# Expert weights in pieces of 4 KB a partition, empty places passed over, and one gate product moved, in a one-core stream step

## The chip, the cores and the metric

The kernel runs on one core of a Trainium2 chip. The metric is the device time of one execution in microseconds (us). The kernel before took 2080.77 us, the median of 3 runs (2078.91 to 2081.96). One further execution was profiled: 2079.63 us by the same clock, with a span of 2077.8 us from its first instruction to its last. All times of single instructions below count from the start of that span.

A core has TensorE (PE, with its weight loads shown apart as PEld), VectorE (DVE), ScalarE (ACT), GpSimd (POOL) and SyncE (SP), which run side by side and wait for each other by semaphores, and 16 DMA engines, which all queues share. SP's transfers run in queue q1, POOL's in queue q0.

## The reference, cut to what matters

One layer over 1,088 tokens of 1,024 features (1,024 tokens of a prompt and 64 of a running stream): a state-space branch and a sparse attention branch, gated and projected, a layer norm, and then the mixture of experts, which is what the change touches:

```python
def moe(x, w_router, router_bias, w_exp_gu, w_exp_down, w_sh_gu, w_sh_down):
    scores = sigmoid(xt @ w_router)
    _, idx = top_k(scores + router_bias, 6)              # 6 of 64 experts a token
    gate = take(scores, idx); gate = gate / gate.sum(-1) * 2.5
    routed = routed_experts(xt, idx, gate, w_exp_gu, w_exp_down)
    shared = swiglu(xt, w_sh_gu, w_sh_down)              # silu(x @ w[:, :256]) * (x @ w[:, 256:]) @ w_down
    return routed + shared

def routed_experts(...):
    # token-slots sorted by expert; each expert's rows padded to whole blocks of 128 rows;
    # each block: swiglu(x_pad[tok], w_exp_gu[e], w_exp_down[e]) * g, added to the tokens' rows
```

An expert has a gate-and-up matrix of 1024 x 512 and a down matrix of 256 x 1024, all float32: 2 MB and 1 MB. There are 1088 x 6 = 6,528 token-slots. They don't fill their blocks: a block of 128 rows holds **places**, and those without a token are empty.

## The kernel before

All activations stay in one large tensor in SBUF, `arena`; names such as `xg`, `ewg` and `x1` are slices of it, so a profile shows them all as `arena`. The program is written out engine by engine, in the order in which each is to work, with the semaphores by hand. There is no scheduler.

**Ahead of the expert loop.** After the first layer norm the routing is counted: `count` and `rank` give each token-slot its number among its expert's; a few small DVE steps turn the counts into the experts' first blocks (`blocks_planned`). Beside that runs the shared expert for each of the 9 token tiles i: PE `shared_up(i)` (L845, 16 matmul instructions), ACT takes silu of the gate half (`hsh`), DVE `gate_shared(i)` (L2186) multiplies it by the up half in PSUM, PE turns the product (`turn_hidden`, L827), ACT copies it, PE `shared_down(i)` (L836), and DVE `add_shared(i)` (L2203) adds it to `x1`. PE's results go to PSUM banks that are handed out in turn; PE may fill a bank only when the reader of its former content is done. DVE's loop over i also does, at i = 0, `slots` for tiles 0 to 4, at i = 1 `slots` for tiles 5 to 8 and `block_and_place`, and from i = 2 to 4 one-hot rows for 54 pairs of a tile and a choice (L2304, L2305); POOL makes a third of each pair's rows (L1277), PE multiplies the rows into a table (L891), `tab`, of 128 places x blocks: token and gate of each place. Twelve buffers hold the one-hot rows.

**Empty places.** A place with no token gets the row number T + partition = 1088 + partition in `tab`. `x1_d` and `acc_d` in DRAM have T + 128 rows, so an empty place reads one of 128 spare rows and adds its (zero-gated) result to one.

**The expert loop** runs over blocks in pairs; buffers are doubled by u = 0, 1, and `last_pair` and the experts of the blocks are read from tables. Per block n:

- SP (`load_gu`, `load_dn`, both by `ld`, so the profile's line is L954) loads the 2 MB for block n + 3 when PE has finished gate-and-up of block n + 1, and the 1 MB for block n + 2 when PE has finished the down product of block n. A partition's share is contiguous in DRAM: 16 KB and 8 KB.
- POOL, in this order: four gathers (L1293) of 128 quarter rows of 1 KB each for block n + 3, by DVE's list `tid`; then `scatter` (L1287), which adds 128 rows of 4 KB to `acc_d`. The scatter waits for both halves of the result (`y_half`) and for the landing of the scatter before it (`y_stored`), since two scatters could add to the same row.
- DVE: the list for the next gather (L2258), the gate-and-up product (L2314), the transposes of the gathered rows (L2264, four), two small columns (L2319, L2320), and one half of the weighting of the result (L2323).
- PE: gate-and-up of block n + 1 (L918, 16 instructions), down of block n (L932, 8), the turn of the hidden rows (L924, 2).

After the loop SP waits for both last scatters, loads `acc_d` back and the second layer norm runs tile by tile.

Of the kernel before, what the change touches and what calls it, by code (L numbers as in the profile page):

```python
# [34 lines left out]
T = SEQ + DEC  # L35
NT = 9
DK = DM // P
# [75 lines left out]
def layer_program(nc, a, out):  # L113
    banks = Banks()
    with ExitStack() as ctx:
# [178 lines left out]
        def s(name):  # L294
            if name not in S:
                S[name] = sem(name)
            return S[name]
# [104 lines left out]
        def _(pe):  # L402
# [531 lines left out]
                    last.then_inc(s(f"edn_full{j}"), 1)  # L934

            pe.wait_ge(s("base_ready"), NT)
            gate_and_up(0, 1, 16)
            turn_eh(0, 1)
            with pe.Fori(0, last_pair) as ip:
                for u in range(2):  # L940
                    n = ip * 2 + u
                    gate_and_up(1 - u, n + 2, ip * 16 + 16 + 16 * u)
                    down(u, n + 1, ip * 16 + 16)
                    turn_eh(1 - u, n + 2)
            gate_and_up(1, last_pair * 2 + 2, last_pair * 16 + 16)
            down(0, last_pair * 2 + 1, last_pair * 16 + 16)
            turn_eh(1, last_pair * 2 + 2)
            down(1, last_pair * 2 + 2, last_pair * 16 + 16)


        @block.sync
        def _(sp):
            def ld(dst, src, name, small=False):
                sp.dma_start(dst, src, allow_slow_non_contiguous=small).then_inc(s(name), 16)  # L954
# [156 lines left out]
                return sp.value_load(brow[0:1, bass.ds(n, 1)], min_val=0, max_val=NE - 1)  # L1111

            def load_gu(e, u):
                ld(ewg[u], a["w_exp_gu"][0, bass.ds(e, 1)].rearrange("a (p k) f -> (a p) k f", k=DK), f"ewg_loaded{u}")

            def load_dn(e, u):
                ld(ewd[u], a["w_exp_down"][0, bass.ds(e, 1)].rearrange("a (p k) f -> (a p) k f", k=2),
                   f"ewd_loaded{u}")

            for u in range(2):  # L1120
                e = expert(u)
# [9 lines left out]
            with sp.Fori(0, last_pair) as ip:  # L1131
                for u in range(2):
# [3 lines left out]
                    load_gu(after, 1 - u)  # L1136
                    sp.wait_ge(s("edn_full1"), n + 1)
                    load_dn(e, u)
            sp.wait_ge(s("ewg_loaded0"), last_pair * 16 + 32)
            for u in range(2):  # L1140
                sp.wait_ge(s(f"y_stored{u}"), last_pair * 16 + 32)
            for i in range(NT):
# [15 lines left out]
        def _(pool):  # L1158
# [125 lines left out]
            pool.wait_ge(s("x1_stored"), 16 * NT)  # L1284

            def scatter(u, rows_):
                pool.indirect_dma_start(acc_d, bass.IndirectOffsetOnAxis(ap=sid[u][:, 0:1], axis=0), rows_, None,  # L1287
                                        compute_op=ALU.add).then_inc(s(f"y_stored{u}"), 16)

            def gather(u):  # L1290

                for g in range(4):
                    pool.indirect_dma_start(xg[u][:, g, :], None, x1_d.rearrange("t (a f) -> (t a) f", a=4),  # L1293
                                            bass.IndirectOffsetOnAxis(ap=tid[u][:, g:g + 1], axis=0)
                                            ).then_inc(s(f"xg_loaded{u}"), 16)

            def carry_wait():

# [382 lines left out]
        def _(dve):  # L1681
# [585 lines left out]

            gate_shared(1)
            dve.wait_ge(s("x1_stored"), 16 * NT)
            for i in range(NT + 1):  # L2270
                if 2 <= i + 1 < NT and i > 0:
                    gate_shared(i + 1)
                if i == 5:
                    await_bank(dve, "tab")
                    dve.tensor_copy(tab[:].rearrange("p a b -> p (a b)"), bank("tab")[:, 0:2 * NBP]
                                    ).then_inc(s("tab_ready"), 1)
                    dve.wait_ge(s("tab_ready"), 1)
                    step(ts(empty, tab[:, 0, :], 0.0, dump[:, 0:1], ALU.is_equal, ALU.mult))
                    stt(tab[:, 0, :], tab[:, 0, :], -1.0, empty, ALU.add, ALU.add).then_inc(s("tab_ready"), 1)
                if i == 6:  # L2280
                    dve.wait_ge(s("tab_ready"), 2)
                    await_bank(dve, "tab4")
                    ts(tab4[:].rearrange("p g n -> p (g n)"), bank("tab4")[:, 0:4 * NBP], 4.0, piece[:, 0:1], ALU.mult,
                       ALU.add).then_inc(s("tab_ready"), 1)
                    dve.wait_ge(s("tab_ready"), 3)
                    list_rows(0, slice(0, 1))
                    list_rows(1, slice(1, 2))
                if i == NT - 1:
                    turn_rows(0, 64)
                    list_rows(0, slice(2, 3))  # L2290
                if i > 0:
                    add_shared(i - 1)
                if i < 2:
                    for j in range(5 * i, min(NT, 5 * i + 5)):
                        slots(j)
                if i == 1:
                    block_and_place()

                for m in planned_in(i):
                    r, k = rows(m // MK), m % MK  # L2300
                    if m >= 12:
                        dve.wait_ge(s("onehot_used"), m - 11)
                    o = onehot[0:r, m % 12, :]
                    ts(o[:, 0:P], iota64[0:r, :], sin_[0:r, m // MK, k:k + 1], None, ALU.is_equal)  # L2304
                    ts(o[:, P + NBP:], iota64[0:r, 0:NBP], sblk[0:r, m // MK, k:k + 1],  # L2305
                       gate[0:r, m // MK, k:k + 1], ALU.is_equal, ALU.mult).then_inc(s("onehot_ready"), 1)
# [103 lines left out]
```

## Time and profile before

| | us |
|---|---|
| median of 3 runs (lowest, highest) | 2080.77 (2078.91, 2081.96) |
| the profiled execution | 2079.63 |
| its span | 2077.8 |
| PE busy in the span | 1959.6 (94%) |
| POOL busy in the span | 618.8 (30%) |
| first gate-and-up starts (block 0) | 1269.47 |
| last gate-and-up starts (block 67) | 2015.12 |
| mean of all DMA over the span | 176 GB/s |

The page's 40 slices show that the DMA engines have a share of 9 or 10 tenths from slice 25 to slice 39, which is the expert loop, and mostly 0 to 4 tenths before. In the views below a row of the timeline gives the start in us, the duration, the engine, the line, what it writes and reads, and in brackets the idle time before it with what ended it. A row of the chain gives start, duration and what the end of the program hung on. A landing time counts from a transfer's issue until its last byte's semaphore.

### The profile page before, as it was taken

To read this page: it belongs to the slowest core of one execution; us is meant where nothing else is said; L and a number is where in the kernel's file an instruction comes from. 1 tells how busy PE (TensorE), PEld (TensorE's weight loads), DVE (VectorE), ACT (ScalarE), POOL (GpSimd) and SP (SyncE) were. 2 spreads that over 40 slices of the span, in tenths; PEclk is the share of its full clock that TensorE was granted. 3 is DMA by queue.
4 is the path that set the end of the run, shared out by engine and by line. 5 is a ranking of instruction groups with operands and counts; after the bars stand their busy time and mean duration, and the time that the engine had idled before them with its cause. 6 is when DMAs were issued, how large, how long until landed. Compare 5 with 4: busy or idle time off the path is not lost.

```text
span 2077.8 us, 23451 instructions
## 1 busy us (share of the span) xinstructions
PE 1959.6 (94%) x7658; PEld 1084.7 (52%) x7658; DVE 929.9 (45%) x2467; ACT 562.7 (27%) x1147; POOL 618.8 (30%) x792
## 2 busy tenths in 40 slices
PE   8998999999999999999999899999999999999990
PEld 6786645666555665556555463444444444444440
DVE  4374465999765533030344743233332332332324
ACT  2223554562566640030233000111111111111114
POOL 0042000101220001101223254545445555555444
PEclk9999999999999999999999999999999999999995
DMA  6031212110110011134211406999999999999995
GB/s 189 3 38 14 64 41 102 41 47 5 26 26 3 1 31 48 44 132 126 103 61 48 155 31 217 376 369 373 381 373 375 378 373 376 375 373 377 375 364 193
DMA packets 130467, 365.09 MB, mean 176 GB/s; under 512 B 34641, under 2 KB 82514, under 8 KB 112594
## 3 DMA queue, kind: packets, MB, share of 16 engines
q1 hardware_dynamic: 105250, 289.80, 37.2%
q0 software_dynamic: 23328, 72.90, 13.6%
q10 hardware_dynamic: 1808, 1.33, 0.2%
q8 instruction: 48, 0.79, 0.2%
q14 instruction: 33, 0.27, 0.0%
HBM read 310.82 MB, written 53.04 MB: 175 GB/s over the span
## 4 chain that ended last, share of the span: by engine, by line
PE 55%; DMA 19%; DVE 8%; issue 7%; POOL 7%; ACT 2%; POOLq 0%; SPq 0%; DVEq 0%; ACTq 0%
DMA arena<-x_d,tid 17%; PE psum L630 11%; PE psum L774 9%; PE psum L792 6%; PE psum L645 4%; POOL arena L1293 3%; PE psum L845 3%; PE psum L444 3%; POOL acc_d L1287 2%; PE psum L479 2%; PE psum L708 2%; ACT arena L1341 2%; DVE arena L2264 2%; DMA acc_d<-arena,sid 2%; PE psum L491 2%
## 5 line engine op out<-in xcount | busy, mean ns | idle before, releaser
L1341 ACT ACTIVATE arena<-psum 128x512 f32<-128x512 f32 (+8 forms) x643 | 286.0, 486 | 1086.6 <-PE psum L918 429.7
L918 PE MATMUL psum<-arena 128*128 128x512 f32 x1088 | 484.3, 598 | 27.8 <-DVE arena L2264 24.9
L918 PEld LDWEIGHTS psum<-arena 128*128 128x128 f32 x1088 | 201.6, 190 | 267.2 <-issue 265.0
L1293 POOL DMA_INDIRECT arena<-x_d,tid x276 | 264.9, 960 | 85.8 <-issue 71.3
L932 PE MATMUL psum<-arena 128*128 128x512 f32 x544 | 244.7, 593 | 0.5 <-ACT arena L1341 0.5
L630 PE MATMUL psum<-arena 128*128 128x384 f32 (+1 forms) x768 | 239.7, 471 | 0.2 <-DMA arena<-in_w_glu 0.2
L2314 DVE TENSOR_TENSOR arena<-arena,psum 128x256 f32<-128x256 f32 x68 | 28.6, 421 | 457.7 <-ACT arena L1341 457.7
L630 PEld LDWEIGHTS psum<-arena 128*128 128x128 f32 x768 | 144.5, 190 | 94.7 <-issue 10.9
L774 PE MATMUL psum<-arena 128*128 128x384 f32 (+1 forms) x576 | 177.7, 472 | 1.1 <-DVE arena L2075 1.1
L2264 DVE STREAM_TRANSPOSE arena<-arena 128x256 f32<-128x256 f32 x272 | 150.3, 610 | 54.7 <-DMA arena<-x_d,tid 53.7
L932 PEld LDWEIGHTS psum<-arena 128*128 128x128 f32 x544 | 103.5, 190 | 130.0 <-issue 129.4
L1915 DVE TENSOR_SCALAR_CACHE_REDUCE arena<-arena 128x512 uint8<-128x512 f32 (+6 forms) x175 | 155.1, 931 | 2.0
L1341 ACT ACTIVATE arena<-arena 128x896 uint8<-128x896 f32 (+4 forms) x120 | 123.0, 1035 | 93.8 <-DVE arena L1961 48.7
L1299 POOL TENSOR_TENSOR carry<-ones 1x1 f32<-1x1 f32 x135 | 53.6, 397 | 313.8 <-DMA acc_d<-arena,sid 279.3
L774 PEld LDWEIGHTS psum<-arena 128*128 128x128 f32 x576 | 110.4, 192 | 67.7 <-issue 2.8
L792 PE MATMUL psum<-arena 128*128 128x512 f32 (+1 forms) x288 | 127.1, 596 | 2.7 <-POOL arena L1251 1.6
L1251 POOL TENSOR_TENSOR arena<-arena 128x384 f32<-128x384 f32 (+1 forms) x24 | 22.8, 951 | 334.2 <-DVE arena L2111 334.1
L1287 POOL DMA_INDIRECT acc_d<-arena,sid x68 | 111.0, 1632 | 11.5 <-POOL carry L1299 10.4
L1341 ACT ACTIVATE arena<-psum,gcol 128x512 f32<-128x512 f32 x68 | 46.7, 687 | 241.3 <-DVE gcol L2320 237.8
L1214 POOL TENSOR_TENSOR arena<-arena,rope 128x72 f32<-128x72 f32 (+3 forms) x72 | 29.5, 439 | 255.0 <-ACT iws L1341 180.8
L1233 POOL TENSOR_TENSOR arena<-arena 128x384 f32<-128x384 f32 (+1 forms) x24 | 23.8, 990 | 267.8 <-DVE arena L2025 267.8
L645 PE MATMUL psum<-arena 128*128 128x512 f32 (+3 forms) x288 | 94.3, 486 | 0.0
(313 smaller groups left out, 2148.1 us busy)
## 6 DMA issues: line engine op xcount, KB each, us to landing
arena<-in_w_exp_gu SPq DMA_DIRECT2D x69, 2048.0 KB, 10.4
arena<-in_w_exp_down SPq DMA_DIRECT2D x68, 1024.0 KB, 10.8
arena<-in_w_in SPq DMA_DIRECT2D x24, 512.0 KB, 4.5
arena<-in_x_prompt SPq DMA_DIRECT2D x10, 512.0 KB, 4.2
arena<-x_d,tid POOLq DMA_INDIRECT x276, 8.8
arena<-in_w_glu SPq DMA_DIRECT2D x16, 256.0 KB, 4.9
arena<-in_w_attn_proj SPq DMA_DIRECT2D x16, 256.0 KB, 4.5
arena<-in_w_out SPq DMA_DIRECT2D x1, 4096.0 KB, 14.4
```

The costliest lines, as they stand in the source:

```text
L444: last = mm(psum[:, b, :], xT[:, k, t:SEQ:BL], w_u[:, k, :], start=k == 0, stop=k == DK - 1)
L630: last = mm(psum[:, b, 0:n], wgs[:, d % 2, w0 + k, :], src[:, k, t0:t0 + n], start=k == 0, stop=k == nk - 1)
L645: last = mm(psum[0:r, b, 0:n], xT[:, k, tok(i)], w_q[:, k, c0:c0 + n], start=k == 0, stop=k == DK - 1)
L774: last = mm(psum[:, b, 0:n], wap[:, w % 2, w0 + k, :], src[:, k, t0:t0 + n], start=k == 0, stop=k == nk - 1)
L792: last = mm(psum[0:r, banks.at[("wo", i)][0] + j, :], g1[:, k, tok(i)], w_o[:, k, j * 512:(j + 1) * 512], start=k == 0, stop=k == DK - 1)
L918: last = mm(psum[:, 2, :], xgT[u][:, k, :], ewg[u][:, k, :], start=k == 0, stop=k == DK - 1)
L932: last = mm(psum[:, 4 + 2 * u + j, :], ehT[u][:, k, :], ewd[u][:, k, j * 512:(j + 1) * 512], start=k == 0, stop=k == 1)
L1287: pool.indirect_dma_start(acc_d, bass.IndirectOffsetOnAxis(ap=sid[u][:, 0:1], axis=0), rows_, None, compute_op=ALU.add).then_inc(s(f"y_sto ...
L1293: pool.indirect_dma_start(xg[u][:, g, :], None, x1_d.rearrange("t (a f) -> (t a) f", a=4), bass.IndirectOffsetOnAxis(ap=tid[u][:, g:g + 1] ...
L1341: return act.activation(dst, src, fn, **kw)
L1915: ins = ts(hits[0:r, 0:n], score(i)[:, 0:n], thr[0:r, g:g + 1], None, op, ALU.add, accum_out=into[0:r, g:g + 1])
L2264: last = dve.transpose(xgT[u][:, :, 32 * g:32 * g + 32], xg[u][:, g, :].rearrange("p (j k) -> p k j", k=DK))
```

## The change

- `load_gu` issues four transfers of 4 KB a partition instead of one of 16 KB, and `load_dn` two of 4 KB instead of one of 8 KB. The semaphores count 64 and 32 a block instead of 16, and PE's and SP's waits are set to that.
- Gathers and scatters get a bound (`bounds_check`): an index above the last token's is passed over without an error. Those are the indices of the empty places. What is gathered for them stays what was in the buffer, and it meets a gate of zero and no scatter.
- `gate_shared(2)` stands in front of DVE's loop over i, and not in its turn i = 1.

```diff
-            gate_and_up(0, 1, 16)
+            gate_and_up(0, 1, 64)
...
-                    gate_and_up(1 - u, n + 2, ip * 16 + 16 + 16 * u)
-                    down(u, n + 1, ip * 16 + 16)
+                    gate_and_up(1 - u, n + 2, ip * 64 + 64 + 64 * u)
+                    down(u, n + 1, ip * 32 + 32)
...
             def load_gu(e, u):
-                ld(ewg[u], a["w_exp_gu"][0, bass.ds(e, 1)].rearrange("a (p k) f -> (a p) k f", k=DK), f"ewg_loaded{u}")
+                w = a["w_exp_gu"][0, bass.ds(e, 1)].rearrange("a (p k) f -> (a p) k f", k=DK)
+                for j in range(4):
+                    ld(ewg[u][:, 2 * j:2 * j + 2, :], w[:, 2 * j:2 * j + 2, :], f"ewg_loaded{u}")
...
             def load_dn(e, u):
-                ld(ewd[u], a["w_exp_down"][0, bass.ds(e, 1)].rearrange("a (p k) f -> (a p) k f", k=2),
-                   f"ewd_loaded{u}")
+                w = a["w_exp_down"][0, bass.ds(e, 1)].rearrange("a (p k) f -> (a p) k f", k=2)
+                for k in range(2):
+                    ld(ewd[u][:, k, :], w[:, k, :], f"ewd_loaded{u}")
...
-            sp.wait_ge(s("ewg_loaded0"), last_pair * 16 + 32)
+            sp.wait_ge(s("ewg_loaded0"), last_pair * 64 + 128)
...
                 pool.indirect_dma_start(acc_d, bass.IndirectOffsetOnAxis(ap=sid[u][:, 0:1], axis=0), rows_, None,
+                                        bounds_check=T - 1, oob_is_err=False,
                                         compute_op=ALU.add).then_inc(s(f"y_stored{u}"), 16)
...
-                                            bass.IndirectOffsetOnAxis(ap=tid[u][:, g:g + 1], axis=0)
-                                            ).then_inc(s(f"xg_loaded{u}"), 16)
+                                            bass.IndirectOffsetOnAxis(ap=tid[u][:, g:g + 1], axis=0),
+                                            bounds_check=4 * T - 1, oob_is_err=False).then_inc(s(f"xg_loaded{u}"), 16)
...
             gate_shared(1)
             dve.wait_ge(s("x1_stored"), 16 * NT)
+            gate_shared(2)
             for i in range(NT + 1):
-                if 2 <= i + 1 < NT and i > 0:
+                if 3 <= i + 1 < NT:
                     gate_shared(i + 1)
```

SP's order in the expert loop, one block of it; `ISA` rows are register and semaphore steps, `in_w_exp_gu` and `in_w_exp_down` the experts' matrices in DRAM. Before:

```order
L954 ISA [waits egu_full]
L954 DMA arena<-in_w_exp_gu 128x4096
L1137 REGISTER_ALU
L954 ISA [waits edn_full1]
L954 DMA arena<-in_w_exp_down 128x2048
```

and with the change:

```order
L954 ISA [waits egu_full]
L954 DMA arena<-in_w_exp_gu 128x1024
L954 ISA
L954 DMA arena<-in_w_exp_gu 128x1024
L954 ISA
L954 DMA arena<-in_w_exp_gu 128x1024
L954 ISA
L954 DMA arena<-in_w_exp_gu 128x1024
L1141 REGISTER_ALU
L954 ISA [waits edn_full1]
L954 DMA arena<-in_w_exp_down 128x1024
L954 ISA
```

Two transfers have become six (the last row's transfer, the second of the down matrix, follows it). They stand behind the same two waits and in the same order. POOL's order is the same in both kernels.

DVE's order behind the block plan (`bexp_i` is the list of the blocks' experts; the 128x256 product is `gate_shared`; the rows of 128x64, 128x384 and `slot` are `slots(0)`). Before:

```order
L2241 TENSOR_SCALAR bexp_i<-bexp 128x1 [waits dve_step]
L2186 TENSOR_TENSOR arena<-arena,psum 128x256 [waits bank_full7,silu_ready]
L2245 TENSOR_TENSOR arena<-arena 128x64 [waits x1_stored]
L2156 TENSOR_TENSOR arena<-iota64,idx 128x384 [waits dve_step]
L2247 TENSOR_TENSOR arena<-arena 128x384 [waits dve_step]
L2248 TENSOR_REDUCE slot<-arena 128x6 [waits dve_step]
```

and with the change, whose lines are numbered six higher there:

```order
L2247 TENSOR_SCALAR bexp_i<-bexp 128x1 [waits dve_step]
L2192 TENSOR_TENSOR arena<-arena,psum 128x256 [waits bank_full7,silu_ready]
L2192 TENSOR_TENSOR arena<-arena,psum 128x256 [waits bank_full0,silu_ready,x1_stored]
L2251 TENSOR_TENSOR arena<-arena 128x64
L2162 TENSOR_TENSOR arena<-iota64,idx 128x384 [waits dve_step]
L2253 TENSOR_TENSOR arena<-arena 128x384 [waits dve_step]
L2254 TENSOR_REDUCE slot<-arena 128x6 [waits dve_step]
```

The product of tile 2, which stood behind the `slots` of tiles 0 to 4 (21 rows further down), now stands ahead of them.

## Rows read from the trace of the kernel before

**Rows 1.** The page's product L2314, once a block; then the windows view of one stretch.
```profile
L2314 DVE TENSOR_TENSOR arena<-arena,psum 128x256 f32<-128x256 f32 x68 | 28.6, 421 | 457.7 <-ACT arena L1341 457.7
...
core 0: us, PE busy (x) PEld busy (x) DVE busy (x) ACT busy (x) POOL busy (x), PEclk, DMA share, GB/s
...
1500.00:1700.00 200.00, 192.55 (x464) 87.08 (x465) 62.51 (x160) 24.18 (x54) 102.56 (x126) 1.00 1.03 376
```

**Rows 2.** Timeline of one block in the middle of the loop, five queues.
```profile
1500.60 7.13 PE L918 MATMUL psum<-arena 128*128 128x512 f32 x16 [0.73 <-DVE arena L2264]
...
1503.54 1.63 POOL L1287 DMA_INDIRECT acc_d<-arena,sid  x1 [0.17 <-issue]
...
1507.90 0.34 SPq L954 DMA_DIRECT2D arena<-in_w_exp_gu  x1
...
1509.29 0.95 POOL L1293 DMA_INDIRECT arena<-x_d,tid  x1 [0.30 <-issue]
1509.48 2.20 DVE L2264 STREAM_TRANSPOSE arena<-arena 128x256 f32<-128x256 f32 x4 [0.87 <-DMA arena<-x_d,tid]
...
1511.81 7.13 PE L918 MATMUL psum<-arena 128*128 128x512 f32 x16 [0.42 <-DVE arena L2264]
```

**Rows 3.** The chain of waits around the same block.
```profile
1492.29 10.82 DMA acc_d<-arena,sid
...
1509.29 11.34 DMA arena<-x_d,tid
```

**Rows 4.** Waits from 1311 to 2014 us: total, times, longest.
```profile
POOL carry L1299 <- DMA acc_d<-arena,sid: 262.6, 63, 5.4
...
PE psum L918 <- DVE arena L2264: 24.5, 42, 1.1
```

**Rows 5.** DMA from 1311 to 2014 us: queue's packets, MB, share; issues, landing.
```profile
q1 hardware_dynamic: 18108, 197.65, 67.0%
q0 software_dynamic: 21085, 65.83, 35.6%
...
arena<-in_w_exp_gu SPq DMA_DIRECT2D x63, 2048.0 KB, 10.4
...
arena<-x_d,tid POOLq DMA_INDIRECT x252, 8.9
acc_d<-arena,sid POOLq DMA_INDIRECT x63, 10.8
```

**Rows 6.** Timeline of PE: gate-and-up of blocks 3, 4 and 67.
```profile
1299.05 7.03 PE L918 MATMUL psum<-arena 128*128 128x512 f32 x16
...
1309.58 2.74 PE L918 MATMUL psum<-arena 128*128 128x512 f32 x6
...
2015.12 7.13 PE L918 MATMUL psum<-arena 128*128 128x512 f32 x16 [0.40 <-DVE arena L2264]
```

**Rows 7.** The chain of waits at block 3: its last gather.
```profile
1306.49 11.59 DMA arena<-x_d,tid
```

**Rows 8.** Loads of `acc_d` in 4 KB rows behind the loop: window, then queue.
```profile
2048.00:2050.00 2.00, 0.00 (x0) 0.00 (x0) 1.66 (x4) 1.71 (x5) 0.10 (x1) 0.50 1.03 422
...
q1 hardware_dynamic: 921, 3.38, 87.3%
```

**Rows 9.** Timeline ahead of the loop: PE around `gate_shared(2)`, and POOL's one-hot rows.
```profile
1171.44 0.68 PE L827 MATMUL psum<-ident,arena 128*128 128x128 f32 x2 [9.49 <-DVE arena L2186]
1171.91 8.35 PE L845 MATMUL psum<-arena 128*128 128x512 f32 x16
...
1181.47 10.76 POOL L1277 TENSOR_SCALAR arena<-iota,sblk,tokid 128x117 f32<-128x117 f32 x13 [35.22 <-DVE sin_ L2254]
...
1190.63 7.28 PE L891 MATMUL psum<-arena 128*128 128x234 f32 x36
```

**Rows 10.** Windows within that gap of PE.
```profile
1168.00:1172.00 4.00, 0.56 (x3) 0.59 (x4) 3.79 (x8) 0.00 (x0) 0.00 (x0) 0.50 0.00 0
```

**Rows 11.** The chain of waits behind the loop: the last two scatters.
```profile
2027.68 6.11 DMA acc_d<-arena,sid
...
2034.21 5.95 DMA acc_d<-arena,sid
```

More of the change, by code:

```diff
@@ L941, in _ @@
                     n = ip * 2 + u
-                    gate_and_up(1 - u, n + 2, ip * 16 + 16 + 16 * u)
-                    down(u, n + 1, ip * 16 + 16)
+                    gate_and_up(1 - u, n + 2, ip * 64 + 64 + 64 * u)
+                    down(u, n + 1, ip * 32 + 32)
                     turn_eh(1 - u, n + 2)
-            gate_and_up(1, last_pair * 2 + 2, last_pair * 16 + 16)
-            down(0, last_pair * 2 + 1, last_pair * 16 + 16)
+            gate_and_up(1, last_pair * 2 + 2, last_pair * 64 + 64)
+            down(0, last_pair * 2 + 1, last_pair * 32 + 32)
             turn_eh(1, last_pair * 2 + 2)
-            down(1, last_pair * 2 + 2, last_pair * 16 + 16)
+            down(1, last_pair * 2 + 2, last_pair * 32 + 32)
         @block.sync
```

## The prediction
> **What bounds the kernel now.** I read the stages first, then one block of the expert loop, then the chain and the waits, and last the DMA queues. The change touches the loop, and the stretch ahead of it by one step. In the loop two things look full at once: PE is busy for 192.55 of 200 us, and the DMA engines' share is 1.03 [rows 1]. They can't both be the cause, and the block shows which is. Gate-and-up starts at 1500.60 and again at 1511.81, a period of 11.21 us, and PE waited 0.42 us for DVE's transposes, which began when a gather had landed [rows 2]. From block 4 (1309.58) to block 67 (2015.12) there are 63 periods, (2015.12 - 1309.58) / 63 = 11.20 us each. The last period before the gathers were late, 1299.05 to 1309.58, took 10.53 us [rows 6]. That is what PE needs when nothing is late; a wait costs more than it shows (24.5 us in all [rows 4]), since matmuls behind a wait also lose the overlap with their forerunners. So DMA takes 0.67 us of each period, 42 us in all.
>
> In the chain POOL issues a scatter when the one before has landed, 10.82 us after 1492.29; then it issues four gathers; and the last, from 1509.29, lands 11.34 us later [rows 3]. POOL stood 262.6 us waiting for scatters [rows 4]. The loop of scatter behind scatter, 10.8 us to landing and some 0.4 us to the next issue, has the period itself: 11.2. It is the queues that make it so long: the last two scatters of the program, with little beside them, took 6.11 and 5.95 us with POOL's own part [rows 11].
>
> Why they wait is in the queues [rows 5]. In 703 us q1 has 125 transfers of 128 partitions, 16,000 packets, and 16 small ones for each: 18,000, near the 18,108 shown. So a packet is one partition's share, 16 KB or 8 KB. In q0, 65.83 MB over 21,085 less 16 for each of 315 transfers, 16,045, are 4.1 KB each. Per block that is 16 packets per engine in q1 and 16 in q0 (8 for the gathers, 8 for the scatter), and both queues have work nearly always: a gather's or scatter's packet stands behind a 16 KB or an 8 KB one in turn. In engine time q1 costs 0.670 x 703 / 197.65 = 2.383 us a MB, all 16 engines together, and q0 0.356 x 703 / 65.83 = 3.80.
>
> **The change part by part.**
>
> *Pieces of 4 KB.* They do two things. A q0 packet now stands behind 4 KB instead of 16 or 8: the wait for each turn falls to a quarter or a half. The weights' own cost changes too: behind the loop, loads whose packets are 4 KB (3.38 MB in 921 packets, 9 x 16 of them small) run at 422 GB/s with a share of 1.03 [rows 8], 1.03 x 2 / 0.844 = 2.44 us a MB. A block's 3.146 MB then cost 7.68 us instead of 7.50: dearer by 0.18.
>
> *Empty places.* The product L2314 ran 68 times [rows 1], so 68 x 128 = 8,704 places hold 6,528 slots, and 25% are empty. No row shows a passed-over index. At best it costs no DMA time: q0's 1.049 MB a block fall to 0.786 and 3.98 us to 2.99. At worst it costs what a row costs now, 3.98. I take 2.99, since the engine time of q0 goes by its packets. POOL may also need time for the comparison. Its indirect transfers take 1.63 and 0.95 us now, and for one block they stand from 1503.54 to 1510.24 with gaps of 0.3 [rows 2]: 6.7 us. Below, nothing changes; above, each takes twice as long (5.4 us more a block). I take nothing on the path: 3.8 us of a 10.53 us period cover it.
>
> *The loop's sum.* DMA time a block: 7.68 + 2.99 = 10.67 us, against 7.50 + 3.98 = 11.48 now. Now 11.48 fit into a period of 11.20 (the shares overlap by 1.026 [rows 5]). With the same overlap, 10.67 needs 10.40 us, and without any 10.67. PE needs 10.53. So the two are nearly equal, and PE is ahead by a hair where the overlap holds. I take 10.60: 63 x (11.20 - 10.60) = **-37.8 us**; the ends are 10.53 (-42.2) and 10.80 (-25), the latter if packets' overlap is lost and blocks with few empty places run late.
>
> What would be late next? The last gather of block 3 was issued at 1306.49 and landed after 11.59 us [rows 7]; PE had its first wait then, and the same gather about 0.8 us sooner would have been in time (DVE waited 0.87 at such a place [rows 2]). So gathers need to land within 10.7 us. With 12 packets of q0 an engine a block instead of 16, each behind 4 KB, and with POOL no longer held by scatters, I expect 4 to 6. Weights: the 2 MB issued at 1507.90 are read two periods less a gate-and-up after that, 2 x 10.53 - 7 = 14 us; they land in 10.4 now [rows 5], and I expect 8 to 12. They are what goes late if the DMA engines don't keep up. SP issues six transfers instead of two at 0.34 us each [rows 2]: 4 x 0.34 plus register steps, under the 3.4 us until its next wait. The semaphore values of PE's waits need one more register step a pair of blocks; PE's sequencer is ahead of its matmuls there, so 0, at most 34 x 0.1 = 3 us.
>
> One rule speaks against this part. The Trainium skill (DMA: Bandwidth & Descriptors, "Measured (HBM→SBUF, 128 partitions, SWDGE, issued from GpSimd)") says to batch transfers to 1 MiB and more for 75% of the peak; pieces of 512 KB would be below. By its fit of some 2 us fixed for each transfer, one after the other, six pieces would need about 19 us a block, an estimate from that page. The rows bear it out little: 512 KB transfers queued behind each other ran at 422 GB/s [rows 8].
>
> *The gate product.* PE's turn of tile 1 waited 9.49 us for `gate_shared(2)` [rows 9], because its PSUM bank was tile 2's. The granted clock fell to 0.50 in that idle stretch, 1.2 GHz [rows 10], and `shared_up(3)` took 8.35 us [rows 9] instead of the 7.03 of a row like 1299.05 [rows 6]. With the change PE goes on at about 1162. But the gain stops at the one-hot rows: they start when the slots are placed, at 1181.47 as before, since DVE has the same work up to there, and POOL takes 10.76 / 13 = 0.83 us for each. The 18th is ready at 1181.5 + 18 x 0.83 = 1196.4. PE finished these 18 at 1190.63 + 7.28 = 1197.9. So some **-1.2 us** remain of the 9.5, from 0 (if PE, waiting between one-hot rows, is given the lower clock again and runs the next products at it) to -1.5.
>
> *Behind the loop.* The last two scatters need landing, one behind the other, 6.11 and 5.95 us. The first waited for one before it and can go about 1 us sooner; each has fewer rows (-25% of the moving part). I take **-2.3 us**, from -1 to -4.
>
> Sum: -1.2 - 37.8 - 2.3 = -41.3. Against the profiled execution, 2079.63 - 41.3 = 2038.3 us. That execution lay 1.1 below the median of the runs, so I give **2039 us**.
>
> **The rivals.**
>
> *DMA stays the bound, with less gain.* For it: 10.67 us of DMA time for a 10.53 us period leaves no slack, and the weights' queue would get less of the engines while q0's packets go in turn with its small ones. Against it: the overlap. With a period of 10.9: 63 x 0.30 = 19, less 3.5: about 2058.
>
> *Passed-over places cost DMA time all the same* (the slower side). The mechanism is the DMA engines' sum in the loop: 7.68 + 3.98 = 11.66 us, by the overlap 11.37, against 11.20. It decides as soon as a passed-over place costs more than some four fifths of a full one. 63 x 0.17 = +11, less 3.5 at the two ends: about 2088. For it: no row shows that a bound drops a packet; against it: the program names fewer rows to move.
>
> *POOL's check of the bound becomes the period.* If each indirect transfer took twice as long, POOL would need 6.7 + 5.4 = 12.1 us a block, 63 x 0.9 = +57: 2137. From 0.9 us more a transfer it is slower than now. A comparison costing as much as the whole address work is not likely.
>
> *The pieces run at a poorer rate.* If 512 KB pieces cost 10% more than 2.44 us a MB, 8.45 + 2.99 = 11.44, by the overlap 11.15: 63 x 0.05 = 3 and the two ends: 2074. It decides from 2.7 us a MB on, and [rows 8] speak against it. That is a mild form of the page's rule above. Its full form, pieces one after another, would be some 500 us slower, an estimate from the page's fit.
>
> **How the numbers follow.** The forecast 0.66, DMA still the bound 0.15, passed-over places at full cost 0.09, POOL 0.03, the poorer rate 0.07 (nearly all of it in the mild form). The forecast's own range is 2030 (10.53 a period, the ends at their best) to 2050. The range for 8 in 10 is 2030 to 2075, which takes in the second case and the mild poorer rate, and leaves out the two slower ones and the tails. A difference of 0.2%, 4 us, is about what can be told from none here. Faster by more than that: 0.66 + 0.15 + about 0.04 of the poorer rate = 0.85; within: 0.03; slower: 0.09 + 0.03 = 0.12.
>
> **What would show each step.** In the changed profile the landing of gathers and scatters should fall to 6 us or less, and POOL's wait for scatters nearly vanish; q0's megabytes in the loop fall by a quarter, its engine time too; q1 cost about 2.44 us a MB; gate-and-up follow each other in 10.5 to 10.7 us with few waits for DVE; and the turn of tile 1 start near 1162 with one-hot rows still starting near 1181. If q0's bytes stay, the second or third rival holds. If PE waits for `in_w_exp_gu` instead of DVE, the weights are late. If the scatters still take 10 us to land, the packets in turn were not why.

## The result, and the profile after

The changed kernel takes 2102.75 us, the median of 4 runs (2101.42 to 2103.9), beside 2080.84 for the kernel before: a ratio of 1.0105, 95% interval 1.009 to 1.0119. It is slower by 1%, where 2039 was forecast. Ratios here and below leave out runs that the chip disturbed and the medians include them, which matters for two of the kernels below: one run of 10 of bounds_only and three of 11 of halves_even were such runs, and without them the medians are 2078.87 and 2084.72. The profiled execution has a span of 2101.0 us, 23.2 more than before.

First the timeline of PE in the changed kernel: the first gate-and-up, those of blocks 4 and 67 that answer to [rows 6], and two where PE waited.

```profile
1266.92 7.13 PE L918 MATMUL psum<-arena 128*128 128x512 f32 x16 [1.38 <-DVE arena L2209]
...
1307.03 7.03 PE L918 MATMUL psum<-arena 128*128 128x512 f32 x16
...
1373.61 7.13 PE L918 MATMUL psum<-arena 128*128 128x512 f32 x16 [1.79 <-DMA arena<-in_w_exp_gu]
...
1385.02 7.13 PE L918 MATMUL psum<-arena 128*128 128x512 f32 x16 [0.62 <-DMA arena<-in_w_exp_gu]
...
2041.93 7.03 PE L918 MATMUL psum<-arena 128*128 128x512 f32 x16
```

The 63 periods from block 4 to block 67 take (2041.93 - 1307.03) / 63 = 11.67 us each, and 11.20 before. That is +29.4 us. Up to block 4 the changed kernel is ahead by 1309.58 - 1307.03 = 2.6 us (1.9 of them before anything that the change moves, as the part on the stretch ahead of the loop shows), and behind the last gate-and-up it is shorter by (2077.8 - 2015.12) - (2101.0 - 2041.93) = 3.6 us. 29.4 - 2.6 - 3.6 = 23.2: the whole difference, and it lies in the loop. What PE waits for has changed: not DVE's transposes, but the weights.

The waits from 1311 to 2014 us, in the changed kernel; they answer to [rows 4].

```profile
POOL carry L1305 <- DVE arena L2330: 216.2, 52, 7.1
...
PE psum L918 <- DMA arena<-in_w_exp_gu: 50.7, 40, 2.7
...
POOL carry L1305 <- DMA acc_d<-arena,sid: 23.8, 8, 3.3
```

POOL's wait for scatters fell from 262.6 us to 23.8: when it comes to a scatter the one before has mostly landed, and it waits for DVE's half of the weighted result (L2330) instead. PE waits 50.7 us for the 2 MB of an expert, and no row of PE's waits names the transposes any more. The DMA queues of the same stretch, beside [rows 5]:

```profile
q1 hardware_dynamic: 52073, 189.63, 72.7%
q0 software_dynamic: 20160, 48.49, 26.9%
issues: line engine op xcount, KB each, median us to landing
arena<-in_w_exp_gu SPq DMA_DIRECT2D x240, 512.0 KB, 7.1
arena<-in_w_exp_down SPq DMA_DIRECT2D x120, 512.0 KB, 10.6
arena<-x_d,tid POOLq DMA_INDIRECT x242, 6.5
acc_d<-arena,sid POOLq DMA_INDIRECT x60, 9.4
```

The reader is to see three things. q0's bytes did fall: 48.49 MB over 703 / 11.67 = 60.2 blocks are 0.805 MB a block, against 1.049. Gathers land after 6.5 us, not 8.9. But q1 now costs 0.727 x 703 / 189.63 = 2.70 us of all engines' time a MB instead of 2.38, and a block's DMA time is 3.146 x 2.70 + 3.14 = 11.62, more than the 11.48 of before. And the sum of the shares is 0.996, where the kernel before had 1.026. (A queue's share times 703 us, over the blocks in 703 us, is the engine time of a block by definition; the sum over both queues, divided by the summed share, therefore always gives back the period. The two things to learn from it are which queue the time is in, and whether the summed share stays.) The windows view of the changed kernel for the stretch shown in [rows 1] says the same: less moved, in engines that look hardly less full.

```profile
1500.00:1700.00 200.00, 183.83 (x440) 82.91 (x439) 58.87 (x153) 22.89 (x51) 101.24 (x119) 0.98 1.00 338
```

The page's POOL row for gathers, which answers the question of the bound's own price (before: 264.9 us busy, 960 ns each):

```profile
L1299 POOL DMA_INDIRECT arena<-x_d,tid x276 | 281.1, 1018 | 86.3 <-issue 80.0
```

### The profile page after: what moved, and what is told of

The parts are those of the page before. It is cut to its first block, busy times and chain, and to the rows that moved or that the text cites. A ratio compares the mean times of both kernels' runs of the same rounds, so it can differ in the third digit from the quotient of the medians.

```text
span 2101.0 us, 24621 instructions
## 1 busy us (share of the span) xinstructions
PE 1963.5 (93%) x7658; PEld 1080.3 (51%) x7658; DVE 923.9 (44%) x2467; ACT 563.0 (27%) x1147; POOL 634.9 (30%) x792
## 4 chain that ended last, share of the span: by engine, by line
PE 70%; DMA 18%; DVE 6%; ACT 2%; issue 2%; SPq 2%; POOL 1%; POOLq 0%; DVEq 0%; ACTq 0%
DMA arena<-in_w_exp_gu 16%; PE psum L918 15%; PE psum L630 11%; PE psum L774 8%; PE psum L792 6%; PE psum L645 4%; PE psum L932 3%; PE psum L444 3%; PE psum L479 2%; ACT arena L1347 2%; PE psum L708 2%; PE psum L845 2%; PE psum L491 2%; PE psum L727 2%; SPq L954 2%
## 5 line engine op out<-in xcount | busy, mean ns | idle before, releaser
L1299 POOL DMA_INDIRECT arena<-x_d,tid x276 | 281.1, 1018 | 86.3 <-issue 80.0
L630 PEld LDWEIGHTS psum<-arena 128*128 128x128 f32 x768 | 144.2, 190 | 94.8 <-issue 10.9
L1292 POOL DMA_INDIRECT acc_d<-arena,sid x68 | 110.9, 1631 | 38.5 <-POOL carry L1305 19.4
L1237 POOL TENSOR_TENSOR arena<-arena 128x384 f32<-128x384 f32 (+1 forms) x24 | 23.8, 992 | 267.5 <-DVE arena L2031 267.5
```

The costliest lines, as they stand in the source:

```text
L630: last = mm(psum[:, b, 0:n], wgs[:, d % 2, w0 + k, :], src[:, k, t0:t0 + n], start=k == 0, stop=k == nk - 1)
```

## The experiments

Two theories went into them. **Theory 1, the pieces:** 4 KB packets cost more engine time than 16 and 8 KB packets, and the loop was bound by engine time already. **Theory 2, uneven relief:** the empty places of a block are its last ones, and in a scatter a place is a partition. If an engine serves fixed partitions, the engines of the low partitions keep all their rows, and a transfer ends with its fullest engine. Its rival is that the average over the engines counts.

Unless said otherwise a kernel's ratio is to the kernel before, run on the same chip. The kernel before took 2082.48 beside gate_only, pieces_only, bounds_only and bounds_spread, 2080.84 beside all_spread, spread_8k, gather_bound and scatter_bound, and 2081.2 beside the rest. Medians from different groups are so compared by their ratios.

**gate_only: the moved product alone.** The diff is the last hunk of the change.

> Only gate_shared(2) moved ahead of the slots; weights and indirect transfers as before. In the changed kernel's trace the first gate-and-up starts at 1266.92 instead of 1269.47. Both theories (the pieces' dearer packets; the uneven relief of the engines) put the loss into the expert loop: here the loop keeps its 11.2 us a block and the time falls by 2.5 us, to about 2078. If it falls by nothing, the gain ahead of the loop was given back in it.

2081.52 us, ratio 0.9992 (0.9982 to 1.0002): no gain that can be told from none. This is the base for all that follows. In its trace the first gate-and-up starts at 1270.39, not earlier than before, so the 2.6 us that the changed kernel had at that point are not to be put down to the moved product alone: two executions with the same moved product start it at 1266.92 and at 1270.39.

**pieces_only: the change without the bounds.**

```diff
-                                        bounds_check=T - 1, oob_is_err=False,
...
-                                            bounds_check=4 * T - 1, oob_is_err=False)
```

> The 4 KB pieces and the moved product, without the bounds: every place is gathered and scattered. Theory 1 (pieces: q1 costs 2.70 us a MB beside the indirect transfers instead of 2.38): DMA time a block 3.146 x 2.70 + 3.98 = 12.5 us, a period of 12.1 to 12.4, so 2135 to 2155. Theory 2 (the pieces cost 2.44 as forecast, the empty places relieve only the engines of the high partitions): 7.68 + 3.98 = 11.66, a period of 11.4, about 2090.

2104.77 us, ratio 1.0103 (1.0086 to 1.012): 23 more than gate_only, and as slow as the changed kernel. Theory 1 had 2135 to 2155 and theory 2 had 2090 for it; it lies between them. The waits are those of the changed kernel already, without any bound:

```profile
POOL carry L1304 <- DVE arena L2329: 252.4, 61, 7.1
...
PE psum L918 <- DMA arena<-in_w_exp_gu: 45.7, 55, 2.0
```

Its queues from 1311 to 2014 us:

```profile
q1 hardware_dynamic: 52513, 191.22, 69.2%
q0 software_dynamic: 20446, 63.84, 34.6%
```

q1 costs 0.692 x 703 / 191.22 = 2.54 us a MB. That lies between the 2.44 of the forecast and the 2.70 of theory 1 as first put. A block's DMA time is 8.00 + 4.00 = 12.0 us, against 7.50 + 3.98 before: what grew is q1's part alone, by 0.50 us. The period grew by less, from 11.22 in gate_only to 11.57, since the shares sum to 1.038 here. 63 x 0.35 = 22 of the 23 us are so in the loop, and in the weights' queue.

**bounds_only: bounds and moved product, weights as before.** The diff is the POOL and DVE part of the change.

> The bounds and the moved product, weights in one transfer of 16 KB and one of 8 KB a partition as before. Theory 1 alone (only the pieces are to blame, empty places save their average share): 7.50 + 0.808 MB x 3.9 = 10.65 us, by the overlap 10.4, so PE's 10.53 to 10.6: about 2040. Theory 2 (empty places are the last of a block, so the scatter's rows on partitions 0 to 63 stay, and a transfer ends with its slowest engine): 7.50 + 1.0 + 2.62 + 0.15 = 11.27, by the overlap 11.0: about 2064.

2079.8 us, ratio 0.9988 (0.9978 to 0.9998). That is 2 us less than gate_only, and the two intervals overlap: no gain of the bounds can be told. Its queues from 1311 to 1970 us:

```profile
q1 hardware_dynamic: 16942, 184.97, 69.2%
q0 software_dynamic: 19610, 46.80, 30.4%
```

The shares sum to 0.996 again with fewer bytes, and PE still waits for gathers; its periods average 11.24. "The average counts" (2040) is out; theory 2 is nearer with 2064, but 16 us too low.

**bounds_spread: the same, with the places of a block dealt over the partitions.** A second list takes the place of 0 to 127 where DVE compares a token's place with the partition; its value at partition c is c6 x 8 + c5 x 16 + (c4 c3 c2) + 32 x (c1 c0), c's bits. Places 0 to 15 so fall on 16 different groups of four partitions.

```diff
+            step(pool.iota(iotap[:], [[8, 2], [16, 2], [1, 8], [32, 4]], base=0, channel_multiplier=0,
+                           allow_small_or_imprecise_dtypes=True))
...
-                    ts(o[:, 0:P], iota64[0:r, :], sin_[0:r, m // MK, k:k + 1], None, ALU.is_equal)
+                    ts(o[:, 0:P], iotap[0:r, :], sin_[0:r, m // MK, k:k + 1], None, ALU.is_equal)
```

> As bounds_only, but a token's place within its block is dealt over the partitions, so that a block's empty places fall on all groups of partitions alike (one 128-value list replaces another in the comparison that makes the one-hot rows; the result is the same). Theory 2: all engines are relieved alike, 10.6 us a block, PE's bound: about 2040, 20 below bounds_only. Theory 1 alone: the same as bounds_only. If it is slower than bounds_only, packets with three rows and one gap cost more than whole packets dropped.

2044.26 us, ratio 0.9813 (0.9783 to 0.9843): 35.5 below bounds_only. Its queues from 1311 to 1970 us:

```profile
q1 hardware_dynamic: 17757, 193.46, 71.8%
q0 software_dynamic: 20570, 49.08, 30.1%
```

By the bytes q0 moves as little as in bounds_only (0.80 MB a block). What differs is that the shares now sum to 1.019, near the 1.026 of the kernel before, and the period is 10.76. Theory 2 reads this as all engines being full together. The relief is still not the whole of what the bytes promise: q0 costs 0.301 x 659 / 49.08 = 4.04 us a MB here, against 3.80, and q1 0.718 x 659 / 193.46 = 2.45, against 2.38.

**spread_only: dealt places without a bound**, the control.

> The moved product and the places dealt over the partitions, without any bound: every place is gathered and scattered, weights as before. Uneven relief: there is nothing to relieve, so 2080 to 2083, as gate_only. If dealing the places is itself of use (order of the rows in memory, fewer rows of one token near each other), it is nearer to bounds_spread's 2044.

2081.22 us, ratio 0.9994 (0.9984 to 1.0004). Dealing the places does nothing by itself.

**halves_even: dealt over the two halves only.**

```diff
-            step(pool.iota(iotap[:], [[8, 2], [16, 2], [1, 8], [32, 4]], base=0, channel_multiplier=0,
+            step(pool.iota(iotap[:], [[1, 2], [2, 64]], base=0, channel_multiplier=0,
```

> As bounds_spread, but dealt over the two halves of the partitions only: place 2c goes to partition c and place 2c + 1 to 64 + c. Empty places then fall on both halves alike, mostly on partitions 48 to 63 and 112 to 127. If an engine serves groups of four partitions in each half (the transfer ends with its fullest engine), half of the engines keep all their rows: 2070 to 2082, as bounds_only. If only the balance of the halves mattered, 2044, as bounds_spread.

2087.52 us, ratio 1.003 (1.0008 to 1.0051). Even a relief that is the same for both halves is worth nothing while half of the groups of four keep their rows. The layout has a second effect, which the expectation did not name: in the kernel's lists a gather puts four quarters of each of 32 places at the same offset in all four 32s of the partitions. As the places lay before, the empty places fill the last gather first, and the gathers' relief is even; with the halves dealt, the empty rows lie mostly in two gathers, at offsets 16 to 31, and their relief is uneven as well. So this kernel is not bounds_only with a better balance, and that it isn't faster than bounds_only is no surprise by theory 2. The Trainium skill (DMA: Bandwidth & Descriptors, "The descriptor swizzle") gives a rule for a plain 1 MiB transfer: the 128 partitions go to the engines in groups of four, and an engine has one such group from each 32 of its half. The three kernels agree with it: bounds_only, halves_even and bounds_spread differ in nothing but which partitions are empty. They don't prove it for indirect transfers: with engines that serve eight neighbouring partitions each, the first two would keep full engines and the third would be even too. The trace itself does not name the engine of a packet, so these times are the evidence, for "an engine serves fixed neighbouring partitions" and not for the size of the group.

**gather_bound and scatter_bound: one of the two bounds at a time**, places as before.

```diff
 # gather_bound: the scatter without its bound
-                                        bounds_check=T - 1, oob_is_err=False,
 # scatter_bound: the gathers without theirs
-                                            bounds_check=4 * T - 1, oob_is_err=False
```

> bounds_only with the bound on the gathers alone; every place is scattered. A gather spreads 32 places with four quarter rows each over the partitions, so passed-over ones relieve all engines alike. Theory uneven relief: 7.50 + 1.0 + 2.62 = 11.1 us, by the overlap 10.85: 2060. If passing over costs as much as it saves (bounds_only won nothing where 2064 was expected), it stays at 2080.

> bounds_only with the bound on the scatter alone; every place is gathered. Theory uneven relief: rows of partitions 0 to 63 are full in most blocks, so their engines keep all of 2.62 us and the period stays: 2078 to 2082. Theory average share (a quarter of the scatter's engine time goes, 0.65 us a block): 2040.

gather_bound took 2072.78 us, ratio 0.9958 (0.9941 to 0.9975), by the ratios 7 less than gate_only: the gathers' relief, even by their layout, is worth something, though less than the 20 expected. Its shares sum to 1.024 from 1311 to 1970 us (0.681 and 0.343). scatter_bound took 2084.37, ratio 1.0015 (1.0005 to 1.0024): the scatter's relief alone is worth nothing. Its queues from 1311 to 1970 us:

```profile
q1 hardware_dynamic: 16683, 182.12, 68.0%
q0 software_dynamic: 19407, 53.29, 32.6%
```

The shares sum to 1.006. The summed share goes with the layout: 1.02 to 1.04 where every place is moved or the relief is even (the kernel before, pieces_only, gather_bound, bounds_spread, all_spread), 1.00 to 1.01 where it is uneven (the changed kernel, bounds_only, scatter_bound).

q1 costs 0.680 x 659 / 182.12 = 2.46 us a MB here, for the same packets that cost 2.38 before. That is not the uneven load alone, since bounds_spread has 2.45. Together with the 16 us that bounds_only missed this stays open: neither its cause nor its size was measured by itself.

**all_spread: the whole change, with dealt places.** The diff to the changed kernel is that of bounds_spread.

> The changed kernel (4 KB pieces, bounds, moved product) with the places dealt over the partitions as in bounds_spread. Theory sum (the loop is bound by DMA engine time, evenly relieved): 3.146 MB at 2.54 us a MB, as in pieces_only, 8.0, and 3.25 for the indirect transfers: 11.25, by an overlap of 1.03 10.9 us a block against 10.76 in bounds_spread: 2054, ten slower than bounds_spread and 48 faster than the changed kernel. Theory turns (once the engines have room, short packets in the other queue let gathers and scatters land in time): PE's 10.53, about 2034.

2057.6 us, ratio 0.9885 (0.9863 to 0.9907): 45 below the changed kernel, and 13 above bounds_spread (15 by the ratios). "Sum" expected 2054 and a period of 10.9, "turns" 2034: short packets in the other queue don't bring the loop down to PE's own time, and the sum comes out within 4 us. Its queues from 1311 to 1970 us:

```profile
q1 hardware_dynamic: 52383, 190.74, 74.8%
q0 software_dynamic: 20214, 48.56, 28.4%
```

A block costs 3.146 x 0.748 x 659 / 190.74 = 8.13 us in q1, at 2.58 us a MB, and 0.80 x 3.85 = 3.1 in q0. The period is (1996.77 - 1309.80) / 63 = 10.90. The expectation had 8.0, 3.25, a summed share of 1.03 and so 10.9, all said before the run from pieces_only and the kernel before: this is the test of the sum as a bound, and it holds for a load that is even. The changed kernel has the same packets of weights, and there q1 costs 2.70 a MB.

**gu_pieces and gu_two: is it the packet or the transfer?** Both start from gate_only and leave the 1 MB whole. In gu_two PE takes the runs in the order in which they lie, and the semaphore counts 32 a block.

```diff
 # gu_pieces: four transfers of 4 KB a partition
+                w = a["w_exp_gu"][0, bass.ds(e, 1)].rearrange("a (p k) f -> (a p) k f", k=DK)
+                for j in range(4):
+                    ld(ewg[u][:, 2 * j:2 * j + 2, :], w[:, 2 * j:2 * j + 2, :], f"ewg_loaded{u}")
 # gu_two: two transfers of 8 KB, each written as two runs of 4 KB
+                w = a["w_exp_gu"][0, bass.ds(e, 1)].rearrange("a (p x y z) f -> (a p) x y (z f)", x=2, y=2, z=2)
+                for x in range(2):
+                    ld(ewg[u].rearrange("p (y x z) n -> p x y (z n)", y=2, x=2)[:, x], w[:, x], f"ewg_loaded{u}")
...
-                    last = mm(psum[:, 2, :], xgT[u][:, k, :], ewg[u][:, k, :], start=k == 0, stop=k == DK - 1)
+                    last = mm(psum[:, 2, :], xgT[u][:, k, :], ewg[u][:, (0, 1, 4, 5, 2, 3, 6, 7)[k], :], start=k == 0, stop=k == DK - 1)
```

> gate_only with the 2 MB of gate and up in four transfers of 4 KB a partition; the 1 MB as before in one of 8 KB. Packet theory: 32 packets of 165 ns and 8 of 318 instead of 8 of 616 and 8 of 318, 7.82 instead of 7.47 us a block; the period grows from 11.22 to 11.45, 2096. It is the base for gu_two.

> As gu_pieces, but in two transfers whose packets are 4 KB too: each reads 8 KB in a row from DRAM and writes them as two runs of 4 KB (PE reads the runs in the order in which they lie). If the size of a packet sets the cost, 2096 as gu_pieces. If the number of transfers does, half of the loss: 2088. If the gap of 12 KB between a piece's rows in DRAM does, 2082.

2099.51 us (ratio 1.0086, 1.0068 to 1.0104) and 2097.68 (1.0082, 1.0064 to 1.01). The queues q1 of both, from 1311 to 1970 us, gu_pieces and then gu_two:

```profile
q1 hardware_dynamic: 41398, 180.62, 68.8%
```

```profile
q1 hardware_dynamic: 39529, 180.53, 68.7%
```

2.51 us a MB in both. 1 MB transfers of 4 KB packets cost what 512 KB transfers of 4 KB packets cost, and reading 8 KB in a row from DRAM saves nothing: it is the size of the packet. Two thirds of the weights' bytes are in 4 KB packets here, and the period of 11.47 in gu_pieces is 0.25 us above gate_only's; in pieces_only, with all bytes in them, it is 0.35.

**spread_8k: bounds_spread with gate and up in two pieces of 8 KB.**

```diff
+                for j in range(2):
+                    ld(ewg[u][:, 4 * j:4 * j + 4, :], w[:, 4 * j:4 * j + 4, :], f"ewg_loaded{u}")
```

> bounds_spread with the 2 MB of gate and up in two transfers of 8 KB a partition; the 1 MB stays one transfer of 8 KB. Theory sum: 24 packets of 318 ns instead of 8 of 616 and 8 of 318: 7.63 instead of 7.47 us a block, so 10.9 instead of 10.76 and 2052. Theory turns: a gather's packet stands behind 8 KB at most, the 19 us of waits for gathers in bounds_spread shrink, about 2034.

2041.77 us, ratio 0.9813 (0.9796 to 0.9829), the same ratio as bounds_spread. The two can't be told apart by these runs. "Sum" had 2052 and "turns" 2034; neither came. The packets of 8 KB did not cost what "sum" charged for them: from 1311 to 1970 us q1 has 195.83 MB at a share of 0.724, which is 2.44 us a MB, beside 2.45 in bounds_spread. Going from 16 KB to 8 KB costs nothing that shows; going to 4 KB does. Its profiled execution was one of its short ones, and PE there, at blocks 4 and 67:

```profile
1307.77 7.03 PE L919 MATMUL psum<-arena 128*128 128x512 f32 x16
...
1976.47 4.03 PE L919 MATMUL psum<-arena 128*128 128x512 f32 x9
```

668.7 / 63 = 10.61 us a period. That is PE's own 10.53 nearly, in an execution 5 us below the median. Both kernels are faster than the kernel before by 1.9%.

## Why the prediction was wrong

**The failed step: "q0's 1.049 MB a block fall to 0.786 and 3.98 us to 2.99".** The bytes fell nearly as said, and so did q0's own time as a mean over 16 engines, to 0.269 x 703 / 60.2 = 3.14 us. The period did not follow, since a mean says nothing of the fullest engine, and theory 2 has a transfer end with that one. The text said "the engine time of q0 goes by its packets" and did not ask whose packets. bounds_only (2079.8, where the mean gives 2040) and bounds_spread (2044.3, with nothing changed but the partitions) show it, with spread_only (2081.2) as the control: 35.5 us were there to be had, but only with the places dealt. In the forecast's own sum: 10.67 us of DMA time with the overlap of 1.026 were to need 10.40; what came is 11.62 with 0.996, so 11.67. The lost overlap is a term that the forecast had at the end of its range, at 10.80 ("if packets' overlap is lost"), without a cause for it.

**The mis-sized term: the pieces at 2.44 us a MB.** It was read from loads behind the loop, with no indirect transfers beside them. In the loop 4 KB packets cost 2.54 (pieces_only), so a block 8.0 us and not 7.68. As the DMA engines were full, most of the 0.50 us above the 7.50 of before went into the period, 0.35 of them: pieces_only lost 23 us to gate_only. The forecast named this as its smallest rival but one ("the poorer rate", 0.07), and cut it at 10% of extra cost with the relief of the empty places still counted. What came was 4% more than forecast by the pieces themselves and no relief. In the changed kernel, with the uneven bounds on top, it was 2.70, the very price from which that rival was to decide; its time (2074) was still 29 us too low, as it counted on the relief. Why q1's price rises from 2.54 to 2.70 there, and only to 2.58 with the places dealt, was not measured by itself.

**What it got right, and why it did not matter.** Gathers land in 6.5 us (4 to 6 was forecast), POOL's wait for scatters fell from 262.6 to 23.8 us, and PE no longer waits for transposes. Scatters still take 9.4 us to land and not 6 or less, so the packets in turn explain only a part of their 10.8. All this would have been a gain only if the engines had had room. The prediction asked which of two full things was the cause and named the loop of scatter behind scatter; pieces_only shows that it was the symptom, since there POOL's wait for scatters is gone from the list and the period is longer. The engines' sum, 11.48 us in 11.20, was the bound, and the prediction had it in its own rows and reckoned the loop by it. What it did not ask is what becomes of shorter turns when the sum rises, and that is what the pieces did.

**PE's and POOL's terms.** The bound costs POOL 58 ns a gather (960 to 1018) and nothing a scatter (1632 to 1631 on the two pages), so POOL is no rival. The extra register step of PE shows nowhere: block 3's period in the changed kernel is 1307.03 - 1296.50 = 10.53, as before.

**Ahead of the loop.** PE's wait of 9.49 us is gone, and the gain stopped at the one-hot rows, as forecast. The changed kernel's timeline:

```profile
1171.01 7.03 PE L845 MATMUL psum<-arena 128*128 128x512 f32 x16
1181.63 5.73 PE L891 MATMUL psum<-arena 128*128 128x234 f32 x16 [3.58 <-DVE arena L2312]
```

PE is done with `shared_up(4)` at about 1178 and starts with the one-hot rows at 1181.63, the time at which they come into being. -1.2 was forecast for it. The changed kernel's trace has -2.6 at block 4 and gate_only +0.9 (1310.49 against 1309.58), since the executions differ already before the moved product. `shared_down(0)` (L836) is the last of PE's work that it can't touch. Before and with the change it starts at:

```profile
1158.25 3.70 PE L836 MATMUL psum<-arena 128*128 128x512 f32 x8 [0.47 <-ACT arena L1341]
```

```profile
1156.36 3.70 PE L836 MATMUL psum<-arena 128*128 128x512 f32 x8 [0.47 <-ACT arena L1347]
```

From there to the first gate-and-up it is 1269.47 - 1158.25 = 111.22 us before, 1266.92 - 1156.36 = 110.56 in the changed kernel and 1270.39 - 1159.85 = 110.54 in gate_only. The moved product is worth 0.7 us, about half of the forecast, and far below what the total times can tell. The other 1.9 us of the changed kernel are that one execution's.

**Behind the loop** -2.3 was forecast and -3.6 measured, even though PE waited 2.66 us there for the last 1 MB. That is inside the -1 to -4 of the forecast, though each side is one execution and a part of the difference may be theirs. The forecast had not named the wait:

```profile
2055.28 3.67 PE L932 MATMUL psum<-arena 128*128 128x512 f32 x8 [2.66 <-DMA arena<-in_w_exp_down]
```

## What to carry to other kernels

Where the DMA share is at 1 through a loop, add up engine time a block by queue and treat that sum as the bound, before any chain of waits: here full engines made the chain of scatters look like the cause, and the pieces, which shortened its waits but added engine time, lost. Work that is left out helps only as much as it relieves the fullest of the 16 engines, as these kernels read, so spread what is left out (here the empty places) so that every group of neighbouring partitions has its share of it; a sum of shares that falls below that of an even load (1.00 against 1.02 to 1.04 here) was the sign that it was not spread. Price a packet size beside the traffic that it will run with, not alone.

## What the runs showed of the hardware

- Cost of a MB in the loop, all 16 engines' time, by packet size: 2.38 us in packets of 16 and 8 KB (kernel before), 2.51 with 4 KB for two thirds of it (gu_pieces, gu_two), 2.54 with 4 KB for all (pieces_only). Behind the loop, with no indirect transfers beside them, 4 KB packets cost 2.44 [rows 8]. With bounds and dealt places 8 KB packets for all cost 2.44 (spread_8k) and 16 and 8 KB ones 2.45 (bounds_spread).
- An accumulating scatter and plain gathers together cost 3.80 us a MB [rows 5], 1.6 times the weights.
- A place that an indirect transfer passes over still leaves a small packet: packets under 512 B from 1311 to 2014 us went from 7,030 to 10,801 in bounds_only, with the same transfers, which is 60 a block, while q0's bytes fell by a quarter. (The changed kernel has 14,033, but its many more transfers of weights bring small packets too.) What they cost was not measured by itself; q0's cost a MB rose from 3.80 to 4.04 us in bounds_spread.
- With bounds in q0 the other queue's packets look longer too: 2.45 us a MB in bounds_spread, 2.46 in scatter_bound and 2.47 in bounds_only for packets that cost 2.38 before; for 4 KB packets 2.58 with the places dealt (all_spread) and 2.70 without (the changed kernel), against 2.54 with no bound (pieces_only).
- Which partitions the left-out rows of an indirect transfer lie on decides what they are worth: the same bounds gave 2079.8 us with the rows as they lay and 2044.3 with them dealt over all groups of partitions.
